# Padding ahead of TensorE's loop over rounds of units: executed as empty instructions in place of being branched over

## The reference, cut to what matters

```python
def _moe(x, w_router, w1, w3, w2):
    logits = (xt @ w_router).astype(jnp.float32)
    top_v, top_e = lax.top_k(logits, TOP_K)          # TOP_K = 2 of N_EXPERTS = 8
    gates = jax.nn.softmax(top_v, axis=-1)
    ...
    def run(args):
        xb, e = args
        return _swiglu(xb, w1[e], w3[e], w2[e])      # 1024 -> 3584 -> 1024
    ...
    y = jnp.zeros((T, D), x.dtype).at[stok].add(yb[dest] * sg[:, None].astype(x.dtype))
```

## Time and profile before

| what | value |
|---|---|
| median of 3 runs | 2643.12 us (2642.01 to 2648.5) |
| the profiled execution's own time | 2646.27 us |
| its span in the profile | 2644.5 us |
| PE busy | 2559.3 us, 97% of the span |
| PE weight load busy | 2164.0 us, 82% |
| DVE busy | 963.9 us, 36% |
| ACT busy | 362.4 us, 14% |
| POOL busy | 42.7 us, 2% |
| mean DMA rate | 230 GB/s |
| mean granted clock of PE | 0.991 |

### The profile page before, as it was taken

How to read it: one execution, slowest core, us unless ns; L and a number is a source line. 1 busy time by engine, 2 the same in 40 slices (tenths; PEclk the granted TensorE clock), 3 DMA queues, 4 the chain that set the end, 5 groups by cost and what they waited for, 6 DMA issues and landing times.

```text
span 2644.5 us, 74267 instructions
## 1 busy us (share of the span) xinstructions
PE 2559.3 (97%) x34014; PEld 2164.0 (82%) x34014; DVE 963.9 (36%) x1799; ACT 362.4 (14%) x836; POOL 42.7 (2%) x74
## 2 busy tenths in 40 slices
PE   8999999889999999999999999998999999999998
PEld 8966778887698477876984778758999999999987
DVE  5663554633477723244676232440000000000002
ACT  1002241210100023401000234020000000000000
POOL 0000000000100000000000000010000000000000
PEclk9999999999999999999999999999999999999999
DMA  6444232004344543325435433387999999999996
GB/s 256 154 137 190 104 141 111 4 27 157 142 172 157 192 162 122 130 112 207 160 121 205 155 118 127 112 296 279 427 427 427 426 427 426 427 425 427 426 425 258
DMA packets 58055, 607.79 MB, mean 230 GB/s; under 512 B 7364, under 2 KB 7492, under 8 KB 12352
## 3 DMA queue, kind: packets, MB, share of 16 engines
q1 hardware_dynamic: 52272, 587.74, 55.8%
q0 software_dynamic: 5648, 18.07, 2.3%
HBM read 599.69 MB, written 6.09 MB: 229 GB/s over the span
## 4 chain that ended last, share of the span: by engine, by line
PE 81%; DMA 14%; DVE 2%; issue 2%; ACT 1%; SPq 0%; POOL 0%; DVEq 0%; ACTq 0%; POOLq 0%
PE bank L313 22%; PE bank L469 16%; DMA slot<-in_experts 13%; PE bank L2616 12%; PE bank L496 7%; PE bank L2629 6%; PE bank L323 5%; PE bank L1652 3%; PE bank L1218 3%; PE bank L1638 1%; PE bank L946 1%; PE bank L1239 1%; DMA arena<-token_rows,arena 1%; PE bank L2021 1%; PE bank L1311 0%
## 5 line engine op out<-in xcount | busy, mean ns | idle before, releaser
L2616 PE MATMUL bank<-arena,slot 128*64 128x84 f32 x14336 | 550.2, 238 | 24.5 <-issue 12.4
L2616 PEld LDWEIGHTS bank<-arena,slot 128*64 128x64 f32 x14336 | 533.5, 138 | 36.2 <-issue 29.5
L313 PE MATMUL bank<-h_cm,slot 128*128 128x256 f32 (+2 forms) x2032 | 446.9, 381 | 1.3 <-ACT h_cm L356 0.6
L313 PEld LDWEIGHTS bank<-h_cm,slot 128*128 128x128 f32 (+2 forms) x2032 | 382.4, 189 | 63.9 <-issue 9.7
L2809 DVE TENSOR_TENSOR ff<-ff,bank 128x168 f32<-128x168 f32 x112 | 36.9, 329 | 660.7 <-PE bank L2616 657.5
L2629 PE MATMUL bank<-ff,arena 128*64 128x84 f32 x5376 | 211.6, 237 | 3.0 <-issue 2.8
L2629 PEld LDWEIGHTS bank<-ff,arena 128*64 128x64 f32 x5376 | 200.9, 137 | 8.3 <-issue 7.1
L469 PE MATMUL bank<-arena 128*128 128x128 f32 x1584 | 187.7, 275 | 0.0
L469 PEld LDWEIGHTS bank<-arena 128*128 128x128 f32 x1584 | 182.2, 192 | 0.0
L323 PE MATMUL bank<-slot,h_cm 128*128 128x512 f32 (+1 forms) x320 | 135.0, 579 | 1.4 <-ACT h_cm L356 1.2
L469 PEld LDWEIGHTS bank<-h_cm,slot 128*128 128x128 f32 x1056 | 125.2, 198 | 9.9 <-issue 9.9
(11 more groups left out here) (441 smaller groups left out, 2564.5 us busy)
## 6 DMA issues: line engine op xcount, KB each, us to landing
slot<-in_experts SPq DMA_DIRECT2D x112, 2048.0 KB, 21.2
arena<-in_experts SPq DMA_DIRECT2D x84, 1024.0 KB, 16.9
slot<-in_ffn SPq DMA_DIRECT2D x22, 2048.0 KB, 8.1
h_cm<-in_experts SPq DMA_DIRECT2D x28, 1024.0 KB, 16.9
slot<-in_ffn SPq DMA_DIRECT2D x22, 1024.0 KB, 5.0
slot<-in_dense SPq DMA_DIRECT2D x11, 2048.0 KB, 7.5
slot<-in_dqk SPq DMA_DIRECT2D x8, 2048.0 KB, 8.6
slot<-in_g SPq DMA_DIRECT2D x8, 2048.0 KB, 8.2
```

Of the source, the lines that this page charges most:

```text
L313: ins = pe.matmul(ps[0:m, j * S:(j + 1) * S], w[:, k * width + c0:k * width + c0 + m], rhs[:, k, :], start=k == 0, stop=k == ks - 1)
L2616: ins = pe.matmul(bank[64 * c:64 * c + 64, m * PLACES:(m + 1) * PLACES], weights[:, c0:c0 + 64], CURRENT[:, k, :], start=k == 0, stop=k == ...
```

## The change

The argument `max_nops=0` goes, and the directive's default for it, 255, takes its place. Padding is never longer than 255 places, so with the default it is never branched over. The place of every instruction in the stream, the alignment of the loop among them, stays as it is.

```diff
@@ -2672,7 +2672,7 @@
                         for t in range(T):
                             ins = pe.transpose(ps[0:PLACES, t * P:(t + 1) * P], WEIGHT[:, t, :], ident)
                     ins.then_inc(gathered, 1)
-                pe.addr_align(256, max_nops=0)
+                pe.addr_align(256)
 
                 with pe.Fori(0, N_EXPERTS // 2) as pair:
                     with pe.Fori(0, 2 * U_EXPERT // RING) as i:
```

## The result

The changed kernel takes 2654.76 us (median of 7 runs, 2651.03 to 2661.32), the kernel before 2645.35 us (median of 7 runs, 2641.96 to 2652.21). The ratio is 1.0041, with a 95% interval of 1.003 to 1.0053: 10.8 us slower, between 7.9 and 14.0 (the two medians by themselves are 9.4 us apart).

A forecast was written before the change was run, and what follows sets the result against it. The stream of weights, started by the loop's first matmul, bounds the kernel; 17.6 us of padding replacing a 4.87 us branch gives +12.7 us, 2659.0 us against the profiled execution, 2655.8 us on the median; range 2641.5 to 2662.5 us.

The forecast's parts named there:

- the likeliest case: Executed padding ahead of the loops delays the end by 12.7 us: 2655.8 us, own range 2649.2 to 2660.2, chance 0.50.
- The number of places: Padding at L2675 in PE's queue, up to the block's end: 218 to 229 places, taken as 220.
- The price of an empty instruction: Each padding instruction costs PE's queue 0.05 to 0.10 us, taken as 0.08; 220 make 17.6 us.
- What is saved: The branch over the padding at L2675 goes, giving back all its 4.87 us, with the block's fetch hidden under the padding.
- rival B: The loops' block is fetched only behind the padding, so nothing is saved: +17.6 us, 2660.7 us; chance 0.17.
- as if the branch had called for it: Reading of the fetch of the loops' block: it came 2.3 us behind the branch at L2675.
- the rule of a taken branch: Skill's rule that a branch out of the two blocks at hand stalls for a fetch, said to agree with 4.87 us.
- The stream follows the first matmul: Whatever shifts the first matmul of L2616 shifts the stream of weights and the end by as much.
- Costs nothing new: PE's clock starts the loop at its lower level already, so a longer rest ahead of it adds nothing.
- Rival A: Empty instructions at L2675 are cheap, 0.02 us or less up to 0.058: no loss, 2640.5 us at best; chance 0.29.
- 62 ns: Skill's time per instruction handled by the sequencer's own program: 13.6 us for the padding, +8.8 us in all.
- the floor of 20 cycles: Skill's least time of an issue, at 1.2 GHz: 3.7 us for 220 empty instructions, -1.2 us in all.

The follow-up runs named there:

- e4: Kernel before with a second padding behind the first, both executed, 474 empty instructions ahead of the loops; ratio 1.0114 to the kernel before.
- e7: The changed kernel measured again, unaltered, beside the kernel before on one chip; ratio 1.0047 to the kernel before.
- e1: Kernel before with the alignment directive deleted, so neither padding nor branch; ratio 0.9995 to the kernel before.
- e10: Kernel before with offset=192 in the directive, 154 places branched over, loops at place 192 of their block; ratio 1.0363 to the kernel before.

## Why the prediction was right

Forecast +12.7 us for the queue and 2655.8 us in all; measured 11.1 us and 2654.76 us, which lies in the range and in the likeliest case's own. That the total is within 1.1 us is in part luck: the kernel before came out 2.2 us higher than the three runs that the prediction started from, and the difference of the medians is 9.4 us (10.8 by the ratio) in place of 12.7.

**The number of places** was counted as 218 to 229 from the matmuls between two restarts; it is 218, the lower end of it. The whole trace bears the count out: between 545.6 us and L2675 there are 56 fetches.

**The price of an empty instruction** was bounded by 0.05 and 0.10 us, taken as 0.08, and is 0.073. The reasoning held roughly: a step less the instruction's own 13 ns is 0.060 us, and for the neighbours it is 0.05 to 0.07 us. The value inside the bounds was a choice of the middle. The sum was 17.6 us and is 16.0.

**What is saved** was taken as 4.87 us on the ground that the block would be fetched by other means. It was: the fetch lay at the start of the padding, the move of L2677 follows the last empty instruction at once, and rival B is out, in the changed kernel, e4 and e7. Two things said on the way there were wrong. The fetch did not come "as if the branch had called for it": e1 has the fetch without a branch, and what goes ahead of it in all kernels is the queue's entry into the block before, at 1777.7 us here. So the rule of a taken branch that the prediction names agrees with the stall of the kernel before, but not with what started the fetch. And the straight code has one stop on "issue" of 1.8 us (L1388), not of about 1 us at the most.

**The stream follows the first matmul**: shown by all kernels but e10 with their 820.4 to 822.9 us. Here the prediction left something out, the first round itself. "Costs nothing new" was said of PE's clock; in this execution the first round came out 1.9 us shorter, 2.3 us being what its time at the lower level accounts for, which is why the span grew by 9.7 us and not by 11.5.

Rival A (cheap instructions) would have needed 0.058 us and is 0.015 us a step away from that; the decision against it rested on PE's own rows against those of instructions that are only handed on. Of the two rules named, the higher one came nearer: the Trainium skill's 62 ns ("TensorE: Matmul & The Clock Gate", Step-by-step: what each phase is for), which the page gives for a matmul alone, against 73, and the floor of 20 cycles ("Runtime: NRT & Kernel Launch", Instruction fetch mechanics) missed. The trace disagrees with it for empty instructions. The same section gives TensorE's instruction memory as 128 KB, eight blocks, and then calls it two cache lines; it spells the two lines out for 32 KB only. Here seven blocks stayed for 28 rounds, so for PE two lines it is not.

## What to carry to other kernels

An instruction that does nothing still takes its turn in the queue: on PE 0.073 us, over five times its own duration. So 218 places of padding that were executed on the way to the critical work cost 16 us, and a padding that is branched over costs 0.2 us, plus the wait for a fetch if the block is not there. Put such a directive where the engine is surely busy or waiting, not behind the last wait, and look at what the engine would have done meanwhile. Without the directive this kernel was as fast (e1, 0.9995), but a loop that drifts to another place can cost more than the padding did: e10 took 3.6% longer from place 192. So count the blocks that a loop touches from where it starts, and try places inside the block too: place 128 gave the fastest version here (0.9975 and 0.9981), faster than both kernels.

## What the runs showed of the hardware

- A NOP on PE's queue: 13 ns long, 0.070 or 0.071 us from start to start in nine cases of ten, 0.073 to 0.076 us on average, since a few steps take up to 0.24 us.
- A taken branch on PE: 0.193 to 0.201 us over padding inside a block, 0.337 us over a border into a block that was there, 4.871 us where it had to wait for its block, and 7.1 to 7.6 us for the way back to the loop's head in e10 where that was gone.
- Loops over seven blocks of 256 instructions ran with no fetch after the first 2.5 us of the second round; in the one kernel where they touch eight, seven rounds of 28 had bursts of nine fetches, and the kernel took 3.6% longer.
- In the first round PE stops at most borders of blocks, for up to 2.6 us at one, 2.2 to 5.8 us in all, depending on the loops' place in their block. Later rounds of the loops over seven blocks have no fetches.
- The fetch of a block began 2.4 to 6.6 us after PE's queue had entered the block before, with the DMA engines busy, and 1.6 to 2.1 us after it where they moved nothing and the queue stood at no wait, with a branch, with empty instructions and with neither. What makes it late is not shown.
